# A one-core fp32 kernel of two transformer blocks: the same steps in a new order on every engine

## What is computed

```python
# first block
h = rms_norm(x, pre_norm_w)
p_rwkv, p_conv, p_pool, p_gate = split(h @ w_in)
y_a = rwkv7_branch(token_shift(p_rwkv), ...)   # 8 heads of 64, a state of 64 x 64 per head, step by step over time
y_b = short_conv_branch(p_conv, conv_w)
y_c = pool_branch(p_pool, pool_w, pool_scale)
merged = sum over n of sigmoid(p_gate[n]) * (y[n] @ w_branch[n])
x = x + rms_norm(merged @ w_out, post_norm_w)
# second block
aq, ak, av, rq, rk, rv, rg = split(rms_norm(x) @ w_in_2)
y_attn = windowed attention with sink (8 heads, 2 key heads, window 128)
y_ret  = silu(rg) * rms_norm(bidirectional_retention(rope(rq), rope(rk), rv))   # 8 heads
x = x + concat(y_attn, y_ret) @ w_out_2
x = x + (silu(m @ w_gate) * (m @ w_up)) @ w_down        # m = rms_norm(x)
```

## Time and profile before

| | before |
|---|---|
| median of 3 runs | 2507.61 us (2503.64 to 2510.13) |
| the profiled execution | 2512.25 us |
| span in its trace | 2510.4 us |
| mean granted TensorE clock | 0.982 |
| busy: TensorE, VectorE, ScalarE, GpSimd | 97%, 44%, 28%, 14% |
| DMA | 160.33 MB, 64 GB/s on average |

### The profile page before, as it was taken

The page is one execution under the profiler, slowest core; times in us unless marked ns, Lnnn a source line. Parts: engine busy times, 40 slices in busy tenths (PEclk is TensorE's granted clock), DMA queues, the critical chain, the costliest instruction groups (busy, mean ns, idle before and its releaser), DMA issues. The chain is left out here.

```text
span 2510.4 us, 31318 instructions
## 1 busy us (share of the span) xinstructions
PE 2441.9 (97%) x13104; PEld 1969.5 (78%) x13104; DVE 1104.0 (44%) x1965; ACT 698.8 (28%) x1146; POOL 359.4 (14%) x270
## 2 busy tenths in 40 slices
PE   8999999999999999999999999999999999999999
PEld 7777777677678888887877777778888888888887
DVE  5755757748732222254365765553222112222223
ACT  4233233232332121233334442432122212211210
POOL 3212213122110002022122112200011001100100
PEclk9999999999999999999999998999999999999999
DMA  4111111112132221333121111142111111111132
GB/s 143 44 52 39 50 50 39 53 51 54 42 117 80 68 80 51 97 97 119 71 60 51 30 34 51 30 122 92 55 47 50 46 51 46 48 50 51 47 115 83
DMA packets 232700, 160.33 MB, mean 64 GB/s; under 512 B 42608, under 2 KB 216304, under 8 KB 232560
## 3 DMA queue, kind: packets, MB, share of 16 engines
q1 hardware_dynamic: 232560, 158.33, 21.3%
HBM read 127.89 MB, written 23.59 MB: 60 GB/s over the span
## 5 line engine op out<-in xcount | busy, mean ns | idle before, releaser
L119 PE MATMUL PS<-Hhi,Whi 128*128 128x512 f32 (+1 forms) x1792 | 571.5, 395 | 2.4 <-DVE Hlo L128 1.3
L119 PE MATMUL PS<-Hhi,Wlo 128*128 128x512 f32 (+1 forms) x1792 | 570.8, 394 | 0.0
L119 PE MATMUL PS<-Hlo,Whi 128*128 128x512 f32 (+1 forms) x1792 | 569.2, 393 | 0.0
L125 ACT ACTIVATE Whi<-Wraw 128x512 fp32r<-128x512 f32 x334 | 209.1, 626 | 1130.5 <-PE PS L119 1125.9
L128 DVE TENSOR_TENSOR Wlo<-Wraw,Whi 128x512 fp32r<-128x512 f32 x252 | 182.1, 723 | 659.5 <-ACT Whi L125 658.9
L119 PEld LDWEIGHTS PS<-Hlo,Whi 128*128 128x128 f32 x1792 | 335.9, 191 | 71.9 <-issue 6.4
L119 PEld LDWEIGHTS PS<-Hhi,Wlo 128*128 128x128 f32 x1792 | 335.0, 191 | 70.0 <-issue 3.7
L119 PEld LDWEIGHTS PS<-Hhi,Whi 128*128 128x128 f32 x1792 | 334.5, 191 | 70.4 <-issue 5.1
L119 PE MATMUL PS<-YMlo,Whi 128*128 128x512 f32 (+1 forms) x720 | 224.2, 387 | 0.0
L119 PE MATMUL PS<-YMhi,Wlo 128*128 128x512 f32 (+1 forms) x720 | 223.4, 386 | 0.0
L119 PE MATMUL PS<-YMhi,Whi 128*128 128x512 f32 (+1 forms) x720 | 223.2, 386 | 0.0
(11 more groups left out here) (291 smaller groups left out, 2824.3 us busy)
## 6 DMA issues: line engine op xcount, KB each, us to landing
Wraw<-in_w_in_dram SPq DMA_DIRECT2D x166, 256.0 KB, 2.9
Wraw<-in_w_gate_dram SPq DMA_DIRECT2D x44, 256.0 KB, 2.9
Wraw<-in_w_up_dram SPq DMA_DIRECT2D x44, 256.0 KB, 2.8
Wraw<-in_w_down_dram SPq DMA_DIRECT2D x32, 256.0 KB, 2.8
Wraw<-in_w_branch_dram SPq DMA_DIRECT2D x24, 256.0 KB, 2.8
yst<-scr_y SPq DMA_DIRECT2D x12, 512.0 KB, 3.8
xs<-in_x_dram SPq DMA_DIRECT2D x8, 512.0 KB, 6.8
scr_y<-cy SPq DMA_DIRECT2D x8, 512.0 KB, 2.6
```

Source lines behind the costliest of these rows:

```text
L119: return self.h.matmul(out, lhsT, rhs, start=start, stop=stop, skip_group_check=True)
L125: return self.h.activation(out, in_, func, **kw)
```

## The change

Only `ORDER` and `PICKS` are replaced. Every letter occurs as often as before in every engine's string, so each engine issues the same steps, and the generators are untouched; where a step stands among the others, and which bank it takes, is new. On TensorE the places at which side products stand alone between dense pairs go from 165 to 177 in stage one and from 93 to 115 in stage two. The last chain step of stage one moves from behind dense pair 1041 to behind pair 1128, the last group norm from 1053 to 1147; the first branch product on its result is pair 1200 in both. The first lines of TensorE's string and of the bank choices:

```diff
@@ -2493,58 +2493,60 @@
 ORDER = {
     "pe":
-        "a5d12a2d13a2d17a2d45a2d9a2d30a2d70p2d2pd10pd20i2dpdid3id16s2d3s2d2p2dsd4pd11pd16i2d21pidid3sd3sd3sd3"
-        "s2d3s2dcdscscd2scsd2cs2cdspcpcsd10gd29sd3sd3sd3sd4sd3sd5csd2cscd2csd3sd4cd2cd2cd2cd11pd3gd10pd17i2dp"
...
+        "a5d14a2d9a2d18ad2ad47a2d6a2d14ad2ad85p2d5pd12pd19i2d3pdid4id10s2d4s2d4p2d3sd6pd9pd18i2d39pid3id5sd4s"
+        "d4sd4s2d4s2d4cs2cd4cs2cd3cs2d2cdspcdpdcsd17gd29pd3sd4spd3sd5s2d5s2d3cpidcd2icd3icd3id4sd6sd4s2d4cs2d"
...
 PICKS = (
-    "0123001123012301230010110101101010101110100101011010101010101010001000000000001010010100101010100010"
...
+    "0123001231012301230010110101010101010101001101001010101101010101010111010100101011111110101010110011"
...
```

More of the change, by code:

```diff
@@ L2501 @@
[L2501 to L2505, removed]
@@ new lines @@
+        "yryd7k2d8y2d4wd22kt2d2rv2d4xr2dkd6kd2rtdktd4xwt2dydykdkd2x2d3tdtd4wx2yd2yd4w2tr2d8tdyr3dtdtdrx2d3ywx"
+        "2kd2y2d6w2x2dkd2wkd135n2d9ndnd17n2d9ndnd17n2d24n2d24n2d37n2d1512o2d21o2d21o2d21o2d21o2d21o2d26o2d19o"
+        "d12o",
+    "act":
+        "w3q2a2qa2q2awa5q3a7w2ewe2wp5w2epwpwes2ws2p3swp2fwpwpfw4fs2ws5wfs6wspsgwfgw2ep4ws2pswes2ps2w2es4ws3p3"
+        "sp2wgwgpwfpw2fw2fs3ws6ws5pswgwfgw2ep2sp2ws2ps2wes2ps2wswes2ws2gp2sp2wpfgwpwpfw4fs3ws6wfs5pswgf2wfgw2"
+        "ep4sws2ps2wes2ps2w2es4wsp2gsp3wfgwpf2pwfw2fw2fwsf2s4wfs6ws4f2wfgwgwf2w2f2sws4wfs2fs3w2fgfwgwtlwbwtbl"
+        "wb2wtw3tw3tw3tw3tw3tw3b2wbwtbw2tw2tw3tw3tw3tw3tw3tw3b2w2tbwbwtw2tw2tw2tw2tw2tw2twmwm2wm2wm2wm2wm2wm2"
+        "wm3n3h2n2h2n2h2n2h2nh2n2h2n2h2n2h2r3w2kwkvwv2kw3k3wowkwv3rwk2wox3y2wxyz2wk2zx2rxr2xrkwryzy2woycyx2kx"
+        "z2kxzwy3zwvycv2x3ry2xywyz2woz2wx2y2xwkz2kxyzr3yrkwrzcz3wozx2k3wx2y3ckyx3wvy2xz2vyvzywzrcwox3y2xzwzy2"
+        "zwk2zr3kr2zwz3wocwk3wvx2v2kxrwkxky2x2yxwoz2yxz2wy2cywx2rx2rykz2dzy2zdywkycwd2w2iwdiwid2i2di3n2h4n2h4"
+        "nh2nh2nh2nh2w2uw2uw2uw2uw2uw2uw2uw2uw2uw2uw2uw2uw2uw2uw2uw2uw2uw2uw2uw2uw2uw2uw2uw2uw2uw2uw2uw2uw2uw"
+        "2uw2uw2uw2uw2uw2uw2uw2uw2uw18uw2uw2uw2uw2uw2uw2uw2uw2uw2uw2uw2uw2uw2uw12",
@@ new lines @@
+    "dve":
+        "Zq2a3qaqaqa5q2j2aqa5j2e2p2sp5ep5i4e2psi3si9pipi9pi9pipip3ip3fpi2fifi10fi17pi2f2i11s2i7s2i5cis2ici4ci"
+        "2s2cs2i2cisi2ci5cpipcgigi4gigi5gfi4fgfi5ep7es2p3s2cicicicis2e2pi6s4i2ci3sci7cpipcgicgi4fpgigi7gipipi"
+        "p2gpip3fpfi28pi2f3i16s2i6s2i4ci3s2ci2fcis4ci4sci7cpipici4cgigi3gigi6gi2fgfep5s2p2s2epcp2s2c2ici3s3ec"
+        "eipi3ci3sici4scgicgi2gigi2pipgi4pi6gi3pipip3ip3fpi2fifi12fi14pi2f2i13s2i6s2i4ci3s2ci3ci2s2csfcsfifcs"
+        "i3ci4cpgipgi4gigi5gi7fgfi5ep5s2p2s2epcp2s2c2ici3s3e2pci3sci4sci7cgpcgpgigi4gpi5fgf2pfpfp3ip3ipi4fifi"
+        "19fif2if2ififi10pi2fifi10s2i7fs2f2s2cf2if2cfis3fcsi2ci2sici4ci4ci4cgigi2fgifgi4gi7gi4fi5fif2ws2wfs2f"
+        "cs2c2s2cwc4gwgfg2fgwgwlwbwlbwb2wtw3tw3tw3tw3tw3twtwtwb2wbwbwbw3tw3tw3tw3tw3tw3twtwtwb3wbwb2wbw13twtm"
+        "twtmwt3wmt2mwt2mwt2mwt2mwtmn5h2n3h2n3h2n2hnhnh2n3h2n3h2n3h2r5w4kwk2wk2wk4wkwok2owr2krkrwrkr3kwx2r2xr"
+        "2yryrxoyrzxzrwoyzrxyr5wzrxzx4r2kr3xr2ywk2y3zy2wkxvxzxkyzxozxky2zoykwzxyr2yzywxvx2yx2r2yryr3y2xwr2zr4"
+        "yzrzr3z2wzxoxywxyozyzxr3zxrwyryxz2r2kr3yr2zwk2vz4xzxkxzwkx2k2owy2oykxzy2r2xvx2ykxkxy2zyzwxy2z2wr3yr3"
+        "zr6xvxrwxryryxzryxzozyxywozr3zyrwrzr2kzr3zr2zwk2z3wkvkwok2owkx3r2x2yr3kr3wkr6kxr3yryx3zy2zkxzkxywxz2"
+        "yoyzyowr3yxvr2yx2zwx2r2xyz2y2zyzdkdyzydwyk2vwd3w2AwdAdwAd2AdAdA3n3hnh3n3hnh3n2h2n2h2n2h2n2h2w2uwuw3u"
+        "wuw3uwuw3uwuw3uwuw3uwuw3uwuw3uwuw19uwuw3uwuw3uwuw3uwuw3uwuw3uwuw3uwuw2uw2uw2uw2uw2uw2uw2uw2uw3uwuw3u"
+        "wuw3uwuw3uwuw3uwuw3uwuw3uwuw2uw2uB3wBwuwB2wuwB2wuwB2wuwB2uB2uBuB",
@@ L2548 @@
+    "0112012012001201010201201201210120120120120120120012012012012012012101021021021001201201201120120120"
+    "1201200121012012012010120120102010210210210210121021021021021001201210100101011021001012100120120120"
+    "120120120120120120120120120120120120120120120120101012301012301012301023"
 )
```

54 lines of the change are left out of this document (16 added, 38 removed).

## The result

The changed kernel takes **2424.76 us** (median of 4 runs, 2423.48 to 2428.33) against 2507.34 beside it: ratio 0.9674, interval 0.9657 to 0.9691. The profiled execution took 2425.92 us, 86.3 less than that of before. The direction and the place of the gain were right, its size was not, and the experiments show that the reason given for the waits held for some of them only.

What follows compares the result with a forecast made beforehand. TensorE was taken as the bound everywhere, with gains only from less standing still and more full clock. The terms summed to −49.8 us, 2512.25 to 2462.5 profiled, so a median near 2458 us; range 2428 to 2490.

Steps and rivals of the forecast that it cites:

- Waits: TensorE's listed waits nearly all go as their steps move back: −27.0 us in stage one, −11.0 in stage two.
- rival C: Waits only move elsewhere and the clock stays; time within 0.3% (7.5 us) of 2507.61 us; chance 0.06.
- Clock: Less time at half clock on TensorE: −9.5 us in stage one, −11.9 in stage two.
- rival A: Narrow side products, not waits, pull TensorE's clock down, so only the waits go: 2479 us; chance 0.20.
- rule of the Trainium skill: On TensorE the full clock does not engage for transposes; by it alone the sum would lose both clock terms.
- the window from 1533.30: Stage two stretch at half clock, TensorE busy 12.58 of 13.50 us, read as a bunch of narrow products without a wait.
- Switching: 37 more side products alone between TensorE's dense pairs cost time, 25 vanished handovers save some: +3.6 us, between 0 and +7.
- The edge: From stage one to the branches, the later last group norm leaves little slack for the branch input: +1.0 us.
- new waits: Each engine's new order may make evacuations stand behind later steps and hold banks: +5.0 us, between 0 and 20.
- Rivals B: Late tail of stage one: branch input transfers stand further back and TensorE waits; up to 2482 us; chance 0.08.
- D: Slower: bank evacuations queue behind ScalarE's weight copies, up to 0.63 us per half tile; 2519 us; chance 0.08.

Runs made afterwards that it cites:

- three edits: Kernel before with VectorE's scan early, TensorE room for A0 and the bonus product in odd units, and group norms' transposes later: 2508.9 us against 2510.1.

## Why the prediction was wrong

The step that failed is the one from a wait to its cure, and with it the size of four terms: waits, clock, switching, and edge with new waits.

*The bound, the place, the direction*: right. TensorE was the bound, only standing still and the clock were to be had, and both came from the two stages named.

*Waits* (−27.0 and −11.0, elsewhere nothing): under-sized. 35.4, 12.9 and 2.9 us went. I left 6.9 and 4.5 us alone because only the large rows were worked through; the small ones went with them, from what cause no run shows. 13 us of the error.

*Why they go* ("a wait of w goes when its step moves back by w"): right for Yt's own waits, wrong as a rule. Each wait was read against its neighbour, and WU's was put down to five pairs that became nine; put back to five in the changed kernel, 0.8 us came back of 6.2; moving two steps of VectorE in the kernel before took 5.7 of its 8.4 us. In the kernel before, moving the steps one wait at a time made the waits move on, as rival C had it: 5.7 us of WU came back as AB, RAV and cu, and 31 us of waits were left after three edits, a third of them at X11t, with 17 us more at half clock. What the odd units lacked was room for the way from A0 to X11t, through VectorE and the transfers. The changed order gives that way 115 to 154 pairs for 83 to 90, and with the room taken back 14.9 us of waits returned. This number stood in the order and was not looked for. The waits on WU in the even units are another matter, VectorE's order; what removed the rest is not shown.

*Clock* (−9.5 and −11.9): 12.4 and 17.2, 8 us of the error. In stage one the reason held: no waits, no stretches, and both came back together when room was taken. I discounted it by a quarter for no reason a row gave (three quarters of 12.4 are 9.3 and half of 23.5 is 11.8, so the two terms are also 0.3 too large). In stage two, rival A's idea that narrow products pull the clock holds for two-column products and fell for transposes; there the full clock was not lost in 8 × 4.5 us of them. The rule of the Trainium skill quoted in the prediction ("TensorE: Matmul & The Clock Gate", Part 4) is not borne out by that run. Nor does the window from 1533.30 fit it, as the prediction read it: what stood just ahead of the fall was a two-column sum, and the transposes came 11 us after it, at half clock already.

```profile
1531.79 2.28 PE L119 MATMUL PS<-cst,rot 128*128 128x2 f32 x16
...
1544.39 1.97 PE L122 MATMUL PS<-cst,rot 128*128 128x128 f32 x8
```

Of the seven stretches of the kernel before in stage two, four begin 1.1 to 3.2 us after the start of such a sum, and the other three stand at waits on inn and qs of 1.7 to 2.4 us. So waits and such sums were both there, and half was taken without telling them apart.

*Switching* (+3.6): should have been nothing. 17 places fewer changed 0.3 or 0.4 us. The prediction set 37 new places against 25 handovers, but these are only the ones between different kinds of side products. With the same steps every new place takes one handover away, so 37 go, 12 of them between products of one kind, like the example in the earlier trace rows; at up to 0.18 us each they pay for the 4 to 7 us. The steps also got some 5 us shorter, which no term had and no run explains. Together 9 us of the error.

*The edge* (+1.0) *and new waits* (+5.0): neither came, 6 us. The branch inputs were in time, and no new kind of wait is in the list. Rivals B and D did not happen.

*The range* ended at 2428, since all listed waits and all of the clock came to 2432 and I allowed a few us for the rest. 6 us of the clock stayed, but 12 us of waits went that were not listed, and some 5 us of shorter steps lay beyond what I had let be negative, although nothing in the rows excluded it.

## What to carry to other kernels

Before a wait is read against the step just ahead of it, follow the longest way through the other engines and back to the bound engine, and count how much work of the bound engine lies along it: if that is shorter than the way, removing a wait between can only move it on, as it did here in the odd units. The changed kernel pays by overlapping the units more deeply, not by moving single steps. And a price for an edit taken from two rows should be tried against the whole: the length of a stage less waits and less lost clock, which came out alike to 0.1 us in two profiles of one kernel, showed that switching cost next to nothing.

## What the runs showed of the hardware

Matmuls of two columns show as a busy TensorE, and yet the clock fell to half behind 4.4 us of them in every one of eight units (61.3 us in all), while 4.5 us of 128 x 128 transposes never had that effect. The same order of instructions had 13.6 us at half clock in stage two in one execution and 6.8 in another, and up to 24 in runs that differ from it in stage one alone; single executions of the kernel before lay up to 20 us apart, with the mean clock between 0.981 and 0.988. A difference of some 5 us between two orders of this kernel can therefore not be read from one profile. Three waits of 3.2 to 3.8 us had 34 us at half clock right behind them with the three edits, where 42 waits of up to 2.7 us had 27 us in the whole of stage one before.
